# A two-layer hybrid transformer block on one core: weight tiles and everything behind them begin 64 bytes further, the projections' activation tiles another 128 bytes

## The reference, cut to what matters

```
for layer in (0, 1):
    h = rms_norm(x, norm_mix[layer])
    x = x + (mixer_a(h) if layer == 0 else mixer_b(h))
    h = rms_norm(x, norm_ffn[layer])
    u = h @ w_up[layer]                       # 1024 -> 2 * 2816
    u = conv_b + sum(conv_w[j] * shifted(u, j) for j in range(3))
    gate, val = split(u)
    x = x + (silu(gate) * val) @ w_down[layer]   # 2816 -> 1024
mixer_a: q, k, v and the index vectors = h @ w_in (1024 -> 3656), q and k normed per head,
         per query the best 128 keys by an index score, softmax with a bias, then @ w_out
mixer_b: latents = h @ w_down (1024 -> 416), q = norm(cq) @ w_uq, k and v = norm(ckv) @ w_ukv,
         rope, softmax over the causal chunks, then @ w_out
```

## The kernel before, in words

| tile | bytes of it | begins before | mod 256 | begins after | mod 256 |
|---|---|---|---|---|---|
| `xT` residual | 16384 | 16512 | 128 | 16512 | 128 |
| `raw` weights as loaded | 16384 | 32896 | 128 | 32960 | 192 |
| `w_hi` | 16384 | 49280 | 128 | 49344 | 192 |
| `w_lo` | 16384 | 65664 | 128 | 65728 | 192 |
| `act` (over it `ckv_hi`, `ckv_lo`, `cq_hi`, `cq_lo`) | 49152 | 82048 | 128 | 82112 | 192 |
| `h_hi` | 16384 | 155840 | 192 | 155904 | 0 |
| `h_lo` | 16384 | 172224 | 192 | 172288 | 0 |
| `kv_hi`, `kv_lo` (over the end of `h_lo`) | 4096 each | 180416, 184512 | 192 | 180480, 184576 | 0 |
| `qT` | 32768 | 188608 | 192 | 188672 | 0 |
| `a_hi` (over `qT`) | 4096 | 188608 | 192 | 188800 | 128 |
| `a_lo` | 4096 | 192704 | 192 | 192896 | 128 |
| `u_in` | 8256 | 196800 | 192 | 196992 | 128 |
| `cv` | 8192 | 205056 | 0 | 205248 | 192 |

## Time and profile before

### The profile page before, as it was taken

The page is one execution under the profiler, slowest core; times in us unless marked ns, Lnnn a source line. Parts: engine busy times, 40 slices in busy tenths (PEclk is TensorE's granted clock), DMA queues, the critical chain, the costliest instruction groups (busy, mean ns, idle before and its releaser), DMA issues.

```text
span 1270.6 us, 17242 instructions
## 1 busy us (share of the span) xinstructions
PE 1230.8 (97%) x6080; PEld 979.4 (77%) x6080; DVE 767.1 (60%) x1337; ACT 547.6 (43%) x933; POOL 212.8 (17%) x262
## 2 busy tenths in 40 slices
PE   7999999999999999999999978999999999999999
PEld 4868886678788888887887856767788888887887
DVE  3577895754766666563337688762775666664334
ACT  5554336653633333332225676652543333342221
POOL 3314243430400000000003572430400000000000
PEclk9999999999999999999999999999999999999999
DMA  6422222213222222213332110012322222222323
GB/s 230 167 92 78 95 67 67 67 35 133 100 100 99 77 104 83 99 50 99 99 99 89 65 35 1 2 34 91 111 97 99 99 99 99 75 74 83 99 87 111
DMA packets 25120, 110.83 MB, mean 87 GB/s; under 512 B 2752, under 2 KB 3136, under 8 KB 17776
## 3 DMA queue, kind: packets, MB, share of 16 engines
q1 hardware_dynamic: 25072, 110.21, 25.5%
HBM read 108.06 MB, written 6.33 MB: 90 GB/s over the span
## 4 chain that ended last, share of the span: by engine, by line
PE 88%; DVE 5%; POOL 2%; issue 2%; ACT 1%; DMA 1%; SPq 0%; DVEq 0%; POOLq 0%; ACTq 0%
PE ps L1714 25%; PE ps L1716 25%; PE ps L1715 24%; PE ps L1475 3%; PE ps L1494 3%; PE ps L1375 2%; PE ps L1363 2%; DVE h_lo L942 1%; DVE xT L1138 1%; PE ps L1458 1%; DVE w_lo L936 1%; PE ps L1358 1%; PE ps L1448 1%; POOL rope_tmp L478 1%; DMA raw<-in_b_w_down 1%
## 5 line engine op out<-in xcount | busy, mean ns | idle before, releaser
L936 DVE TENSOR_TENSOR w_lo<-raw,w_hi 128x1024 fp32r<-128x1024 f32 (+4 forms) x114 | 194.6, 1707 | 258.4 <-ACT w_hi L570 258.4
L1716 PE MATMUL ps<-h_hi,w_lo 128*128 128x512 f32 (+1 forms) x712 | 280.9, 394 | 0.0
L1714 PE MATMUL ps<-h_hi,w_hi 128*128 128x512 f32 (+1 forms) x712 | 277.9, 390 | 2.2 <-DVE w_lo L936 2.2
L1715 PE MATMUL ps<-h_lo,w_hi 128*128 128x512 f32 (+1 forms) x712 | 279.6, 393 | 0.0
L570 ACT ACTIVATE w_hi<-raw 128x1024 fp32r<-128x1024 f32 (+4 forms) x124 | 177.6, 1432 | 234.0 <-PE ps L1716 233.8
L1714 PE MATMUL ps<-a_hi,w_hi 128*128 128x512 f32 x480 | 189.2, 394 | 1.9 <-DVE w_lo L936 1.4
L1715 PE MATMUL ps<-a_lo,w_hi 128*128 128x512 f32 x480 | 187.9, 391 | 0.0
L1716 PE MATMUL ps<-a_hi,w_lo 128*128 128x512 f32 x480 | 187.7, 391 | 0.0
L1714 PEld LDWEIGHTS ps<-h_hi,w_hi 128*128 128x128 f32 (+1 forms) x712 | 133.5, 188 | 33.6 <-DVE w_lo L936 3.1
L1715 PEld LDWEIGHTS ps<-h_lo,w_hi 128*128 128x128 f32 (+1 forms) x712 | 133.6, 188 | 31.4 <-issue 0.4
L1716 PEld LDWEIGHTS ps<-h_hi,w_lo 128*128 128x128 f32 (+1 forms) x712 | 133.7, 188 | 27.5 <-issue 0.6
(11 more groups left out here) (189 smaller groups left out, 1524.3 us busy)
## 6 DMA issues: line engine op xcount, KB each, us to landing
raw<-in_f_up SPq DMA_DIRECT2D x44, 1024.0 KB, 4.8
raw<-in_f_w_down SPq DMA_DIRECT2D x44, 512.0 KB, 3.4
raw<-in_a_in_wide SPq DMA_DIRECT2D x13, 1024.0 KB, 5.0
bias_tiles<-bias_rows SPq DMA_DIRECT2D x1, 4096.0 KB, 19.8
raw<-in_a_w_out SPq DMA_DIRECT2D x8, 512.0 KB, 3.3
raw<-in_b_w_out SPq DMA_DIRECT2D x8, 512.0 KB, 3.4
xT<-in_xt SPq DMA_DIRECT2D x4, 512.0 KB, 5.7
toep_b<-bias_tiles SPq DMA_DIRECT2D x8, 256.0 KB, 2.7
```

The lines of the kernel that those rows point to most:

```text
L936: dve.tensor_tensor(w_lo[:, s, 0:n], raw[:, s, 0:n], w_hi[:, s, 0:n].bitcast(F32), ALU.subtract)\
L1714: pe.matmul(dst, s_hi, m_hi, start=start, stop=False)
L1715: pe.matmul(dst, s_hi, m_lo, start=False, stop=False)
L1716: return pe.matmul(dst, s_lo, m_hi, start=False, stop=stop)
```

## The change

A filler of 16 words stands behind `xT`, one of 32 words before `a_hi`, and the filler `pad_q` is 32 words shorter, so that what lies behind `diag` moves by 64 bytes and not by 192. No instruction, wait, shape or order of the program is changed; the instructions have other addresses.

```
         xT = sb("xT", [P, KD, S])
+        sb("pad_w", [P, 16])
         raw = sb("raw", [P, 2, SLOT])
         w_hi = sb("w_hi", [P, 2, SLOT], F32R)
         w_lo = sb("w_lo", [P, 2, SLOT], F32R)
...
         with ExitStack() as scope:
             qT = sb("qT", [P, 16, S], F32, scope)
+        sb("pad_a", [P, 32])
         a_hi = sb("a_hi", [P, 2, S], F32R)
         a_lo = sb("a_lo", [P, 2, S], F32R)
         u_in = sb("u_in", [P, 4, S + 4])
         cv = sb("cv", [P, 4, S])
         rbc = sb("rbc", [P, S])
         diag = sb("diag", [P, T, P])
-        sb("pad_q", [P, 16 * S - (4 * S + 4 * (S + 4) + 4 * S + 2 * S)])
+        sb("pad_q", [P, 16 * S - (32 + 4 * S + 4 * (S + 4) + 4 * S + 2 * S)])
```

## The result

The changed kernel takes 1277.5 us (median of 10 runs, 1275.5 to 1279.3), the kernel before beside it 1272.9 us (10 runs, 1270.8 to 1276.1). The ratio is 1.0033, 95% interval 1.0023 to 1.0043: slower by 4.6 us by the medians and by 4.2 (2.9 to 5.5) by the ratio. 1279.5 us was predicted, in a range of 1268 to 1286. Lines of `kernel.py` stand two further down than before (L1714 is L1716 now, and so on).

The account below looks back on a forecast made before the run. TensorE's gapless matmuls were taken to bound the kernel. Out and down projections +6.4 us, all else nothing, on the profiled 1272.42 us gave 1278.8; carrying over the runs' median 0.7 higher gave 1279.5 us, range 1268 to 1286.

Parts of the forecast that it names:

- What bounds the kernel: Up and down projections: TensorE has no gap, so time is the number of matmuls times the distance between starts, 0.2289 us.
- The main step: Out and down projections: moving minus stationary place goes from +64 to -64, mixer A's pair; 1440 matmuls, 228.9 to 233.3 ns.
- Up projections and mixer A unchanged: Up projections and mixer A's input projection: address differences stay +64 and -64, so 228.9 and 233.3 ns stay, no time change.
- The size: Whole kernel: +6.4 us, all from the out and down projections, whose bounds were -3.2 and +12.8 us.
- My own sign of being wrong: Wrong if the down projection does not slow by 3 to 6 ns a matmul, or any other stage changes over 1 us.
- The side readings: Short stretches (heads, index projection, mixer B): difference 0 costs 232 ns, 416 columns turn the sign round, the round is 256 bytes.
- rival B: Up, down and out projections: the stationary operand's place alone decides, 3552 matmuls lose 4.4 ns, +15.8 us, 1288.9 us; chance 0.09.
- A: Whole kernel: nothing happens, mixer A's 233.3 ns comes from its roles, the rest from rounding; 1273.1 us; chance 0.11.
- C: Down and out projections: the round is longer than 256 bytes, so they get faster, -3.2 us, 1269.9 us; chance 0.12.
- D: Absolute place decides: up projections -4.7 us, mixer A -3.0, a tiles +6.4, 1271.8 us, or 1262 with cheap a tiles; chance 0.12.

Follow-up runs that it names:

- a128: Second filler alone against the kernel before: a_hi, a_lo and what lies up to pad_q 128 bytes further, w unmoved; 1276.2 us, ratio 1.0030.
- w64: First filler alone against the kernel before: everything behind xT, the a tiles too, begins 64 bytes further; ratio 1.0006.
- h256: 256 bytes of filler before h_hi against the kernel before, places modulo 256 unchanged; 1272.4 us in one run.
- x0_y0: 192 bytes of filler before h_hi against the kernel before, so w, h and a all stand at 128 modulo 256; 1263.2 us, ratio 0.9926.
- x0_y96: Fillers against the kernel before: h at w's place modulo 256 bytes, the a tiles 96 bytes beyond w's; 1270.1 us in one run.
- x32_y0: Fillers against the kernel before: h 32 bytes beyond w's place modulo 256 bytes, the a tiles at w's place; 1281.3 us in one run.
- a64: The a tiles alone 64 bytes further than in the kernel before, 128 bytes from w modulo 256; 1275.1 us in one run.
- lo128: Against the kernel before, w_lo shifted 128 bytes against w_hi, all behind it by 256; 1282.2 us in one run.
- lo64: Against the kernel before, w_lo shifted 64 bytes against w_hi, h and a at 128 modulo 256; 1279.9 us in one run.

## Why the prediction was right, and where it was not

*What bounds the kernel* held: in every one of the dense stages TensorE has no gap and the distance of two starts is the time.

*The main step* held in place, sign and size for each matmul: y goes from +64 to -64, mixer A already showed that pair, and the down projections went from 228.9 to 233.3 ns (after, a128). That it is the difference of the two places and neither place alone, which the rows could only suggest, w64 and a128 show. *Up projections and mixer A unchanged*: 875 matmuls in 200 us and 13.53 us for 58 distances, both as before. The two long stretches together were to take 4.7 us more and took 4.4, each out projection 0.85 and took 0.7.

*The size* was put at 6.4 us and is 4.6 by the medians (2.9 to 5.5). Two terms of it are measured. The four stages lose 5.8 us and not 6.4: 4.4 ns is right for the down projections, but in the out projections the distance before is 229.3 and 229.4 ns (184 gapless distances each), so the step there is 4.0; and 18 of the distances hold waits or other matmuls, which took 9.5 us in all before and 9.2 after and are not lengthened by the step. The up projections are 0.3 us shorter together. That makes 5.5, the upper end of the interval; the remaining 0.9 us isn't settled, and a128, whose profile loses as much in these stages, falls further short (3.8 us by the ratio). A candidate can be seen in mixer B's down projection, which took 25.6 us in the profile of before and 22.9 in that of after. Windows of TensorE there, before and then after:

```profile
688.00:714.00 26.00, 21.67 (x110) 0.93 0.25 81
```

```profile
693.00:719.00 26.00, 22.94 (x126) 1.00 0.25 81
```

In the first TensorE waits 3.03 us for `w_lo`, behind the load of the weights, and then has 3.4 us at the half clock (mean granted clock 0.93); in the second it waits 1.76 us and keeps the clock. w64 and h256 run at the distances of the kernel before and took 22.9 us there. Six of the fourteen profiles took 24.5 to 25.8: in each of them TensorE had waited 2.0 to 3.1 us for `w_lo` and the granted clock fell 7 to 8 us into the stage; in the other eight the wait was 1.7 to 1.8 us and the clock stayed. The two kernels with all down projections slow by -64 are among the eight, but so are w64 and h256, and one profile for each kernel can't tell whether slow down projections make it rarer. The mean granted clocks of all runs say a little more: 0.9963 in the 10 runs of the kernel after and in the 6 of a128, 0.9954 in 27 runs of the kernel before (beside w64 and x0_y0), and among those 27 a clock higher by 0.001 goes with a time shorter by 0.5 us. By that estimate some 0.5 of the 0.9 us is the clock; it is not shown.

*My own sign of being wrong* came up: no other stage was to change by more than 1 us, and the index projection (+1.10) and mixer B's down projection (-2.69) did, with two more stages at +0.95 and +1.00. The sign was badly chosen, since w64 shows such changes with every distance as before.

*The side readings* were the weak part. From the earlier trace rows I read that a difference of 0 costs something between the other two; six matmuls in a stage full of waits don't show a steady distance. x0_y96 and x0_y0 have 226.7 ns at 0. From the earlier trace rows I read, for the expectation of x32_y0, that +32 is still cheap and only places further down are dear; +32 is as dear as -64. The surplus of 13.3 ns of the earlier trace rows, also with a difference of 0, was the right hint, and I took it only as the end of a range. The earlier trace rows were right about the round: h256 confirms it. But they showed the sign turned round, and I explained that by the place where the stream of 416 columns ends, 128 bytes further in its round. x0_y0 contradicts this. There the difference is 0 at the start and 128 at the end for even k, 128 and 0 for odd k. Mixer B's down projection, t=1, k = 4, 5, 6, 7:

```profile
697.78 0.35 PE L1715 MATMUL ps<-w_hi,h_hi 128*128 128x416 f32 x1
...
698.34 0.36 PE L1715 MATMUL ps<-w_hi,h_hi 128*128 128x416 f32 x1
...
698.91 0.35 PE L1715 MATMUL ps<-w_hi,h_hi 128*128 128x416 f32 x1
...
699.47 0.36 PE L1715 MATMUL ps<-w_hi,h_hi 128*128 128x416 f32 x1
```

Three matmuls take 0.56 us with 0 at the start and 0.57 with 0 at the end (558 and 568 ns in the trace), so here the end doesn't decide; in the kernel before (0.56 us at -64, 0.57 at +64 at the start) the start doesn't. What sorts 416 columns is open, and the map holds for 512 columns alone. Against rival B the prediction had rows 7, which it misread, and rows 9, of which only the split within one stationary place stands. So that the up projections would stay was right, but with more luck than the working says. The predicted value stood on the two long, equal stretches, and these alone would have carried it; the picture of a smooth slope around it was false, and by it a reader would have placed x32_y0 and x0_y96 the wrong way round.

*The rivals.* A (nothing happens) is out with the interval; the formula of the Trainium skill's page "TensorE: Matmul & The Clock Gate", section "Back-to-back issue gap", 215.8 ns for 512 columns, fits none of the distances, from 226.5 ns up. The page gives it for an isolated matmul and without a word on addresses; for a stream with weight loads it gives about 131 ns, which no stretch here shows either. B (the stationary place) is out with w64, C (a longer round) with h256 and with the down projection after, D (the absolute place) with w64 and a64.

That what meets is the reading of the moving operand and that of the weights is still only argued. The map needs both addresses, and the distance is the same through 200 us in which ScalarE and VectorE come and go; but no run took the weight loads away, and the rows of the loads don't lengthen: 188 ns on average at -64 (after) and at 0 (x0_y0), and lo128 and lo64 show that the three matmuls don't add up pair by pair. The two rows, after and then x0_y0:

```profile
L1716 PEld LDWEIGHTS ps<-a_hi,w_hi 128*128 128x128 f32 x480 | 90.2, 188 | 25.9 <-DVE w_lo L938 2.1
```

```profile
L1715 PEld LDWEIGHTS ps<-a_hi,w_hi 128*128 128x128 f32 x480 | 90.1, 188 | 23.8 <-DVE w_lo L937 2.4
```

## What to carry to other kernels

When a matmul of 512 fp32r columns, each with its own weight load, stands more than 14 ns above its columns divided by the clock, look at where the two operands begin: here beginning both at the same place modulo 256 bytes brought 0.7% for one filler of 192 bytes, and 16 bytes off lost most of it. Compare long stretches without gaps (dozens of starts) before reading anything from a difference of 2%, and count matmuls in equal windows of the two profiles: that shows 0.2% of a stage where the medians of ten runs barely show it of the whole. Check such a layout after every edit that adds or resizes a tile, since each shifts all tiles behind it.

## What the runs showed of the hardware that I had not expected

At 512 columns the cost is not smooth in the difference of the addresses: 227 ns at 0, 229 at +64, and 232 to 234 at all other places tried (+16, +32, +96, 128, -96, -64, -32). The same code at the same addresses can run at two levels: with 128 bytes of difference layer 0's up projection had 232.5 ns and layer 1's 233.3, and with `w_lo` shifted layer 0's down projection had 228.8 and layer 1's 233.6. And the place of the low part counts beside that of the high part: shifting `w_lo` alone by 128 bytes cost the up projection all of the 4.4 ns, though only one of three matmuls has it stationary; layer 0's down projection, with the same differences, lost nothing.
